# Expert results through DRAM rows, fetched once per token, in place of a one-hot scatter per expert

## The reference

```python
def _moe(h, w_router, w_gu, w_down):
    logits = jnp.einsum('bld,de->ble', h, w_router, preferred_element_type=jnp.float32)
    top_v, top_i = lax.top_k(logits, TOP_K)
    gates = jax.nn.softmax(top_v, axis=-1)
    comb = jnp.sum(jax.nn.one_hot(top_i, N_EXPERTS, dtype=jnp.float32) * gates[..., None], axis=-2)
    comb = comb.astype(h.dtype)
    out = jnp.zeros_like(h)
    for e in range(N_EXPERTS):
        out = out + comb[..., e:e + 1] * _swiglu(h, w_gu[e], w_down[e])
    return out
```

## Time and profile before

| | us |
|---|---|
| median of 3 runs (2141.97 to 2211.37) | 2142.83 |
| span of the profiled execution, first to last instruction | 2134.9 |
| median less span | 7.9 |
| PE busy in the span | 1923.1 (90%) |
| DVE busy | 1290.0 (60%) |
| ACT busy | 1091.2 (51%) |
| POOL busy | 130.0 (6%) |

### The profile page before, as it was taken

One profiled execution on the slowest core, in us unless ns is written; L12 is line 12 of the kernel. 1 busy time (PEld: TensorE's weight loads), 2 busy tenths in 40 slices (PEclk: granted clock), 3 DMA queues, 4 the chain that ended last, 5 costly groups with the idle time before them and its releaser, 6 DMA issues.

```text
span 2134.9 us, 27761 instructions
## 1 busy us (share of the span) xinstructions
PE 1923.1 (90%) x10133; PEld 1481.8 (69%) x10134; DVE 1290.0 (60%) x1580; ACT 1091.2 (51%) x1493; POOL 130.0 (6%) x202
## 2 busy tenths in 40 slices
PE   4778899989999989998799999999898989999992
PEld 3456676768888868776767576677677767777771
DVE  4754655553433262465366556588787868697775
ACT  3756533333332233563155445477676757676661
POOL 3010000000000050240000000000000000000001
PEclk7979995689999979998599999999999999999996
DMA  8946640024443444223067667699898979798871
GB/s 283 327 163 222 214 133 11 19 82 122 125 128 119 125 122 128 79 52 109 11 196 229 212 178 236 201 304 319 277 326 272 323 264 331 263 322 302 289 274 36
DMA packets 197611, 412.39 MB, mean 193 GB/s; under 512 B 16428, under 2 KB 35940, under 8 KB 197472
## 3 DMA queue, kind: packets, MB, share of 16 engines
q1 hardware_dynamic: 188928, 394.31, 55.9%
q0 software_dynamic: 8544, 16.14, 2.7%
HBM read 409.10 MB, written 4.33 MB: 194 GB/s over the span
## 4 chain that ended last, share of the span: by engine, by line
PE 73%; DVE 13%; ACT 6%; issue 4%; DMA 3%; POOL 0%; SPq 0%; ACTq 0%; DVEq 0%; POOLq 0%
PE ps L513 19%; PE ps L515 17%; PE ps L514 17%; DVE wlo L486 5%; PE ps L926 3%; DMA rawb<-in_mod_w 3%; PE ps L1096 2%; PE ps L1185 2%; ACT whi L482 2%; PE ps L958 2%; DVE wlo L463 2%; ACT whi L458 2%; PE ps L936 2%; PE ps L1201 1%; PE ps L1141 1%
## 5 line engine op out<-in xcount | busy, mean ns | idle before, releaser
L463 DVE TENSOR_TENSOR wlo<-rawb,whi 128x1024 fp32r<-128x1024 f32 x224 | 272.3, 1236 | 344.5 <-ACT whi L458 343.4
L486 DVE TENSOR_TENSOR wlo<-rawb,whi 128x1024 fp32r<-128x1024 f32 x288 | 347.5, 1222 | 173.9 <-ACT whi L482 172.6
L458 ACT ACTIVATE whi<-rawb 128x1024 fp32r<-128x1024 f32 x224 | 232.1, 1056 | 352.4 <-PE ps L515 319.4
L482 ACT ACTIVATE whi<-rawb 128x1024 fp32r<-128x1024 f32 x288 | 304.3, 1061 | 164.7 <-PE ps L515 87.1
L486 DVE TENSOR_TENSOR wlo<-rawx,whi 128x1024 fp32r<-128x1024 f32 x240 | 290.2, 1222 | 88.4 <-ACT whi L482 87.6
L513 PE MATMUL ps<-whi,eT_hi 128*128 128x512 f32 (+1 forms) x768 | 308.3, 401 | 31.9 <-issue 25.7
L482 ACT ACTIVATE whi<-rawx 128x1024 fp32r<-128x1024 f32 x240 | 252.6, 1061 | 119.0 <-PE ps L515 58.9
L514 PE MATMUL ps<-wlo,eT_hi 128*128 128x512 f32 (+1 forms) x768 | 292.3, 381 | 2.5 <-issue 2.5
L515 PE MATMUL ps<-whi,eT_lo 128*128 128x512 f32 (+1 forms) x768 | 291.0, 379 | 0.0
L513 PE MATMUL ps<-whi,hT_hi 128*128 128x512 f32 (+1 forms) x672 | 261.1, 389 | 20.9 <-DVE wlo L463 17.1
L515 PE MATMUL ps<-whi,hT_lo 128*128 128x512 f32 (+1 forms) x672 | 256.8, 382 | 0.0
(11 more groups left out here) (301 smaller groups left out, 2500.3 us busy)
## 6 DMA issues: line engine op xcount, KB each, us to landing
rawb<-in_od_moe_w_gu SPq DMA_DIRECT2D x192, 512.0 KB, 4.9
rawx<-in_od_moe_w_gu SPq DMA_DIRECT2D x160, 512.0 KB, 5.4
rawb<-in_mod_w SPq DMA_DIRECT2D x96, 512.0 KB, 5.5
rawb<-in_od_moe_w_down SPq DMA_DIRECT2D x96, 512.0 KB, 4.9
rawx<-in_od_moe_w_down SPq DMA_DIRECT2D x80, 512.0 KB, 4.9
rawb<-in_ev_ffn_w_gu SPq DMA_DIRECT2D x44, 512.0 KB, 3.7
rawb<-in_od_w_qkv SPq DMA_DIRECT2D x24, 512.0 KB, 3.9
rawb<-in_ev_w_in SPq DMA_DIRECT2D x22, 512.0 KB, 3.7
```

The lines of the kernel that those rows point to most:

```text
L458: nc.scalar.activation(whi[:, r, :], rawb[:, s, :], ACT.Copy).then_inc(hi_done, 1)
L463: nc.vector.tensor_tensor(wlo[:, r, :], rawb[:, s, :], whi[:, r, :].bitcast(F32), ALU.subtract).then_inc(lo_done, 1)
L482: nc.scalar.activation(whi[:, moe_slot(i), :], moe_raw(j), ACT.Copy).then_inc(hi_done, 1)
L486: nc.vector.tensor_tensor(wlo[:, moe_slot(i), :], moe_raw(i % EB), whi[:, moe_slot(i), :].bitcast(F32), ALU.subtract).then_inc(lo_done, 1)
```

## The change

The result of every expert goes to a DRAM scratch `rows_out`, the same way as the over rows. Each expert has PITCH = 416 rows there. ACT copies y once (`yr`, full float32), POOL stores it (512 KB), and at the end six indirect DMAs fetch for every token its two rows, all in bounds, two for each tile t, with a semaphore for each tile. DVE multiplies by the two weights and adds. Gone are `y_hi_t`, `y_lo_t`, `ohT`, `comb`, the six scatters and their additions, the transposes of `oh`, and the clearing of `acc`. The one-hot and the gather of the next expert move to earlier blocks, and the gather behind the last expert is dropped. New is that POOL clears the part of the scratch kept for more than 160 tokens, by 16 stores of 512 KB from a cleared `h[:, 0, :]`, issued once the rows of the dense SwiGLU's input have been transposed; DVE waits for them before it adds that SwiGLU's result to `x`.

```diff
-        SCATTER = {b: i for i, b in enumerate((4, 6, 8, 13, 15, 17))}
-        OH_TURN = GB + 5
-        ONE_HOT = GB + 10
-        GATHER = {GB + 12: 0, GB + 14: 1}
+        ONE_HOT = GB
+        GATHER = {GB + 8: 0, GB + 10: 1}
...
+            pool.wait_ge(tin_ps, 18)
+            nc.gpsimd.memset(h[:, 0, :], 0.0).then_inc(zeroed, 1)
+            pool.wait_ge(zeroed, 1)
+            for e in range(E):
+                for p in range(XT):
+                    o = e * PITCH + CAP + p * P
+                    pool.dma_start(rows_out[o:o + P, :], h[:, 0, :]).then_inc(zero_out, 16)
...
             for e in range(E):
+                o = e * PITCH
+                pool.wait_ge(y_ev, e + 1)
+                pool.dma_start(rows_out[o:o + P, :], yr[:, :]).then_inc(yr_out, 16)
                 pool.wait_ge(yo_ev, e + 2)
                 for g in range(4):
-                    pool.dma_start(over[e * OV:(e + 1) * OV, g * 2 * P:(g + 1) * 2 * P],
+                    pool.dma_start(rows_out[o + P:o + CAP, g * 2 * P:(g + 1) * 2 * P],
                                    yo[g * OV:(g + 1) * OV, :]).then_inc(yo_out, 16)
+            pool.wait_ge(yr_out, 16 * E)
             pool.wait_ge(yo_out, 64 * E)
+            pool.wait_ge(x_done, 1)
             pool.wait_ge(routed, 2)
-            for c in range(2):
-                for t in range(T):
-                    pool.indirect_dma_start(oy[:, c, t, :], None, over,
-                                            bass.IndirectOffsetOnAxis(ap=orow[:, c, t:t + 1], axis=0),
-                                            bounds_check=E * OV - 1, oob_is_err=False).then_inc(oy_in, 16)
+            for t in range(T):
+                for c in range(2):
+                    pool.indirect_dma_start(oy[:, c, t, :], None, rows_out,
+                                            bass.IndirectOffsetOnAxis(ap=orow[:, c, t:t + 1], axis=0)).then_inc(oy_in[t], 16)
...
                 def begin(b):
-                    if b in SCATTER:
-                        scatter_last(e, SCATTER[b])
-                    if b == OH_TURN:
+                    if b in GATHER and e + 1 < E:
                         pe.wait_ge(e_flo, e * NS + NS)
-                        for m in range(T):
-                            mm = nc.tensor.transpose(ps[:, 6, m * P:(m + 1) * P], oh[:, m, 0:P], ident)
-                        mm.then_inc(oht_ps, 1)
-                    if b in GATHER:
-                        pe.wait_ge(oht_ev, e + 1)
                         pe.wait_ge(oh_v, e + 2)
                         gather(GATHER[b]).then_inc(ga_ps, 1)
...
-            for i in range(6):
-                scatter_last(E, i, within=False)
-            pe.wait_ge(sc_v, E * 6 + 6)
+            pe.wait_ge(y_ev, E)
...
             def take_y(e):
                 act.wait_ge(pe_used, B_MOE + HL + e * EB)
-                nc.scalar.activation(y_hi_t[:, :], ps[:, 4:6, :].rearrange("p a n -> p (a n)"), ACT.Copy).then_inc(y_hi, 1)
+                if e > 1:
+                    act.wait_ge(yr_out, 16 * (e - 1))
+                nc.scalar.activation(yr[:, :], ps[:, 4:6, :].rearrange("p a n -> p (a n)"), ACT.Copy).then_inc(y_ev, 1)
...
+            take_y(E)
             take_over(E)
-            take_y(E)
...
-                    if b == Y_LAST:
-                        split_y(e)
-                    if b in SCATTER:
-                        scattered(e, SCATTER[b])
-                    if b == ONE_HOT:
-                        dve.wait_ge(oht_ev, e + 1)
+                    if b == ONE_HOT and e + 1 < E:
+                        dve.wait_ge(go_ps, e + 1)
                         one_hot(e + 1)
-                    if b in GATHER:
+                    if b in GATHER and e + 1 < E:
                         gathered(GATHER[b], e * 2 + 3 + GATHER[b])
...
+            dve.wait_ge(zero_out, 16 * XT * E)
...
             for t in range(T):
-                for c in range(2):
-                    chain(nc.vector.scalar_tensor_tensor(out=acc[:, t, :], in0=oy[:, c, t, :], scalar=gk[:, c, t:t + 1],
-                                                         in1=acc[:, t, :], op0=ALU.mult, op1=ALU.add))
+                dve.wait_ge(oy_in[t], 32)
+                chain(nc.vector.tensor_scalar(acc[:, t, :], oy[:, 0, t, :], gk[:, 0, t:t + 1], None, ALU.mult))
+                chain(nc.vector.scalar_tensor_tensor(out=acc[:, t, :], in0=oy[:, 1, t, :], scalar=gk[:, 1, t:t + 1],
+                                                     in1=acc[:, t, :], op0=ALU.mult, op1=ALU.add))
```

More of the change, by code:

```diff
@@ L56 @@
 XT = 2
-FAR = 1 << 20
+PITCH = CAP + XT * P
 MOD_CH, MOD_STEP = 12, 3
@@ L395, in build @@
         m_ld = [sem(f"m_ld{i}") for i in range(RM)]
-        y_hi = sem("y_hi")
-        y_lo = sem("y_lo")
+        zeroed = sem("zeroed")
+        zero_out = sem("zero_out")
+        y_ev = sem("y_ev")
+        yr_out = sem("yr_out")
         e_sg = sem("e_sg")
@@ L406, in build @@
         yo_out = sem("yo_out")
-        oy_in = sem("oy_in")
+        oy_in = [sem(f"oy_in{t}") for t in range(T)]
         x_oh = sem("x_oh")
-        x_go = sem("x_go")
+        x_go_pe = sem("x_go_pe")
+        x_go_act = sem("x_go_act")
         x_xp = sem("x_xp")
@@ L1106, in gather_over @@
                 return mm
-            def scatter(m, half):
-                o = ps[:, 6 + half, :]
-                yc = slice(512 * half, 512 * (half + 1))
-                nc.tensor.matmul(o, ohT[:, m * P:(m + 1) * P], y_hi_t[:, yc], start=True, stop=False)
-                return nc.tensor.matmul(o, ohT[:, m * P:(m + 1) * P], y_lo_t[:, yc], start=False, stop=True)
-            def scatter_last(e, i, within=True):
-                if i == 0:
-                    pe.wait_ge(y_lo, e + 1)
-                if i == 4 and within:
-                    pe.wait_ge(e_flo, e * NS + 1)
-                if i > 1 or not within:
-                    pe.wait_ge(sc_v, e * 6 + max(i - 1, 0))
-                scatter(i // 2, i % 2).then_inc(sc_ps, 1)
             def expert(e, more):
@@ L2070, in extra @@
                     conv(b)
-                dve.wait_ge(x_yhi, at(1, 1))
-                nc.vector.tensor_tensor(y_lo_t[:, :], ps[:, 4:6, :].rearrange("p a n -> p (a n)"),
-                                        y_hi_t[:, :].bitcast(F32), ALU.subtract).then_inc(x_ylo, 1)
-                for i in range(6):
-                    m, half = i // 2, i % 2
-                    cols = slice(512 * half, 512 * (half + 1))
-                    dve.wait_ge(x_sc, at(6, i + 1))
-                    nc.vector.scalar_tensor_tensor(out=acc[:, m, cols], in0=ps[:, 6 + half, :],
-                                                   scalar=comb[:, m, bass.ds(e + 1, 1)], in1=acc[:, m, cols],
-                                                   op0=ALU.mult, op1=ALU.add).then_inc(x_scv, 1)
             def route():
@@ L2102, in route @@
                 chain(nc.vector.tensor_copy(om[:, 1, :, :], m2[:, :, :]))
-                for t in range(T):
-                    chain(nc.vector.tensor_scalar(m1[:, t, :], m1[:, t, :], rt[:, 3, t:t + 1], None, ALU.mult))
-                    chain(nc.vector.scalar_tensor_tensor(out=comb[:, t, 1:], in0=m2[:, t, :], scalar=rt[:, 4, t:t + 1],
-                                                         in1=m1[:, t, :], op0=ALU.mult, op1=ALU.add))
+                chain(nc.vector.tensor_copy(gk[:, :, :], rt[:, 3:5, :]))
                 dve.wait_ge(pos_ps, 1)
```

113 lines of the change are left out of this document (33 added, 80 removed).

## The result

The changed kernel takes 2167.9 us (median of four executions, 2163.7 to 2170.4), against 2142.8 before. The ratio, with the two executions of the kernel before at 2211 left out, is 1.011 (95% interval 1.008 to 1.013): slower by 1.1% where 1.8% faster was forecast, 64 us above the forecast and outside its range. The profiled execution took 2163.72 with a span of 2162.0; before, 2134.9.

What follows compares the result with a forecast made beforehand. PE was taken to bound heavy experts and the down projection, PE and DVE light experts' blocks 0 to 20. Savings 6.1 + 17.75 + 9.55 + 0.4 + 4.6 = 38.4 us take 2142.8 to 2104; range 2093 to 2118.

Steps and rivals of the forecast that it cites:

- Clearing 8.4 MB: Stores of zeros during the dense SwiGLU, where PE is busy throughout: 34 us, all hidden, cost 0.
- The median above the span: Whole run: the median lies 7.9 us above the profiled span, an offset the change was said not to touch.
- heavy: Experts 0 and 1, which run the over rows: PE alone decides, 3.05 us saved each, 6.1 for both.
- light expert: Experts 2 to 7: each saves 3.55 us, 3.2 up to block 20 and 0.35 in the down projection.
- blocks 5 to 12: Light experts, two scatters and additions gone: 0.95 us saved, bounds 0.66 and 2.2.
- `one_hot` moved, first gather: Light experts' down projection: PE's wait for `oh` goes, a stall at block 47 may come; net 0, within 0.4.
- last expert, from its first `eg`: The last light expert saves 3.55 us and both useless gathers, 9.55 in all.
- router, norm 3 to the first `eg`: A chained clearing and a small operation leave DVE's path: about 0.4 us saved.
- sum starts earlier: Tail: DVE waits for two fetches instead of six, so the sum starts 2.8 us earlier.
- three one-input operations: Tail: one two-tensor operation per tile becomes one-tensor, 0.6 us saved each, 1.8 in all.
- Loads: Rival in the experts: weight loads become the bound; 2114 us in mild form, 2126 in full; chance 0.11.
- The rival of slow fetches: Tail: six fetches of valid rows set the end, 2109 us, at worst 2194; chances 0.08 and 0.04.

Runs made afterwards that it cites:

- the early Exp: One tiny unused Exp on ACT in the last QKV blocks: changed kernel 2098.6 to 2108.7 us (four), 2164 (two); kernel before 2200.9 to 2212.5.
- the filling in all waits: Small unread matmuls before every wait for exponentials in attention 1: changed kernel 2120.8 to 2127.1 us, ratio 0.991; kernel before 2170.5, 1.010.

## Why the prediction was wrong

**The step that failed** is "Clearing 8.4 MB ... Cost 0", with the silent assumption that a stage which the change doesn't touch keeps its time. Within its own stretch the step was right: from attention 0's last score product to norm 2, a stretch that holds the dense SwiGLU and the clearing, the profiles take 358.7 us (after) and 360.1 (kernel before with the clearing), and without it 360.0 (before) and 361.7 (clearing late). DMA view of after, and windows of its whole length:

```profile
rows_out_scratch<-h POOLq DMA_DIRECT2D x16, 512.0 KB, 10.3
```

```profile
460.00:480.00 20.00, 17.29 (x72) 13.30 (x71) 9.98 (x12) 6.88 (x9) 9.38 (x17) 0.87 0.67 249
480.00:500.00 20.00, 20.00 (x90) 16.57 (x89) 5.73 (x6) 8.16 (x9) 0.00 (x0) 1.00 0.88 329
500.00:520.00 20.00, 20.00 (x97) 16.62 (x95) 8.82 (x10) 5.22 (x6) 0.00 (x0) 1.00 0.39 108
```

It is over by 500 us, in some 34 us as estimated, and PE is busy for 20.0 of 20 us beside most of it. What it cost came 380 us later: attention 1 at clock 0.52, 59.9 us, and 4.7 more in the projection behind it. Shown is that the clearing at that place, alone, takes the high level from the kernel before (0 of 6 high-clock, against 10 of 12 when placed later and 54 of 79 without it), and that taking it away or moving it gives the changed kernel high-clock executions again (6 of 8, 4 of 8, against 0 of 10). Shown too is that more work for TensorE all through attention makes the level safe (18 of 18 executions of the four kernels with 51 or more extra matmuls there, 18 of 18 of the three with 28). The clearing shifts the odds and doesn't decide by itself: with the early Exp the changed kernel has the high clock in 4 of 6 although it clears at the old place, and the kernel before loses it in 6 of 6 without any clearing.

Not settled is by what path a transfer at 466 us reaches the clock at 878. No engine waits for it. But there is a row ahead of attention that goes with the level. These are the first 17.8 us behind the start of norm 2, some 100 us before attention 1, in the kernel before, the same with the clearing, and the changed kernel:

```profile
762.25:780.05 17.80, 14.26 (x43) 10.77 (x44) 10.91 (x12) 5.46 (x7) 13.59 (x20) 0.50 0.43 119
```

```profile
768.32:786.12 17.80, 13.58 (x50) 10.50 (x51) 10.91 (x12) 5.46 (x7) 13.50 (x21) 0.65 0.53 148
```

```profile
760.28:778.08 17.80, 13.49 (x50) 10.46 (x51) 10.91 (x12) 5.45 (x7) 13.40 (x21) 0.66 0.54 147
```

In the first the clock stays low all the while; in the other two it comes up once for a moment and falls again. Of the ten profiles with neither the early Exp nor the filling in all waits, the three with 0.50 here have attention 1 at the high clock and the seven with 0.63 to 0.66 have it at the low. With the early Exp it is the other way round (0.66 and high, 0.50 and low), and the filled kernels are high with either. That looks like theory A, an upstream edit that moves the moments at which the clock changes against the work, but it is one profile for each kernel, and no run set such a moment on purpose. The cause on this path stays open.

**The median above the span.** "7.9 above that span, which the change doesn't touch" is no property of the kernel: each execution lies 1.7 to 2.0 above its own span (2163.72 and 2162.0), and the rest was the difference between executions. It cost nothing here, since high-clock executions of the kernel before have medians of 2142 to 2150 by session, but the reason given was wrong.

**The other terms**, by the two profiles, from norm 3 on, where 38.4 was forecast. The pair gives 34.0. Over the profiles of seven versions of the kernel before and twelve of the changed one the medians are 1133.1 and 1096.1: 37.0. The changed kernel with the early Exp has 1091.9: 37.9 less than before. That this comes so near to 38.4 is in part luck: as the table shows, the first expert and the tail gave less than forecast, the router more, and the light experts more for a reason that the sum doesn't have.

| step | predicted | measured |
|---|---|---|
| expert 0 to expert 1 (heavy) | 3.05 | -2.8 in this pair (169.0 to 171.8); 163.5 to 171.8 in all profiles, by the length of a stretch at clock 0.5 inside it |
| expert 1 to expert 2 (heavy) | 3.1 | 2.8 (153.3 to 150.5) |
| light expert | 3.55 | 4.4 (583.8 to 561.9 over five); 4.1 by the medians of all profiles |
| blocks 5 to 12 | 0.95 | 0.64, the lower bound |
| blocks 13 to 20 | 1.73 | 1.73 |
| `one_hot` moved, first gather | 0 | +0.64 - 0.43 = 0.2 saved |
| last expert, from its first `eg` | 9.05 | 6.9 in this pair (94.5); 8.5 (101.4 to 92.9) between executions without the slip of 1.5 us named at the end |
| router, norm 3 to the first `eg` | 0.4, and 0.45 of expert 0's first scatter | 4.0 in this pair (76.7 to 72.7), 2.5 by the means of all (75.0, 72.5) |
| sum starts earlier | 2.8 | 0.5 |
| three one-input operations | 1.8 | 1.4 |
| behind the sum | 0 | -0.6 |

The three rows below "light expert" are parts of it.

- *Light experts.* The mechanism holds: even distances and PE's ring as the limit. DVE's part in blocks 5 to 12 was hidden altogether, so the lower bound was the value. The first gather's 0.64 was PE's wait for `oh`, as supposed, and the stall at block 47 is 0.43: they nearly cancel, as counted, though the stall is a little beyond the 0.4 named as a sign of being wrong. Ahead of the first `eg`, where `y_lo_t` and block 4's scatter went and 0.5 was taken, an undisturbed expert saves 0.4 (9.33 to 8.91 from its first product). All this makes 3.3. The rest of the 4.1 is no work removed: the distance between the last two copies of `eg` is 13.0 in place of 11.5 us in 26 of 42 light experts of the kernel before and in 19 of 72 of the changed one, some 0.5 us on the mean, and longer stretches ahead of the first `eg` (12.28 in one expert of before) are rarer too. Why, no run shows. The 5 us in which PE waits for its instructions are still 4.3 to 5.4.
- *Loads.* The rival is out: 0.90 of DMA, 314 GB/s and no wait, though POOL's store of y now stands in the same stretch. The turns between queues that the Trainium skill describes under "DMA: Bandwidth & Descriptors", section "Queues, rings and completion order", don't show in the time here: gate and up loads land in 5.3 and 5.6 us by their medians over the run, against 4.9 and 5.4 before, well inside the ring's lead of an estimated 12.
- *Router.* The gain is there at either level of attention 1 (low-clock: 76.5 in the kernel before with the clearing, 72.7 in the changed one). It has three parts. DVE comes to the one-hot 0.7 sooner (39.98 and 39.26 us behind norm 3), where 0.4 was taken. The scatter in front of expert 0's block 4 goes, 0.45. And in the gather of the over rows PE waited for its instructions twice in the kernel before and once in the changed one, a wait that the prediction didn't have:

```profile
1055.73 0.85 PE L1104 MATMUL ps<-oh,h 128*128 128x32 f32 x6 [2.45 <-issue]
1058.97 8.96 PE L1104 MATMUL ps<-oh,h 128*128 128x32 f32 x42 [2.39 <-issue]
```

```profile
1115.99 9.37 PE L1104 MATMUL ps<-oh,h 128*128 128x32 f32 x48 [2.12 <-issue]
```

  The second wait, 2.1 to 2.4 us, is in four of the seven profiles of the kernel before and in one of twelve of the changed one; what brings it is not shown.
- *Tail.* The last product ends at 2117.61 and the first fetch is issued at 2125.96, 8.35 later, against 5.97 before: 2.4 more, where 1.3 was taken. The stores that have to land took 4.13 instead of 2.96. The fetch of valid rows took 5.39, against 3.01 for one of dropped rows: 2.4 more, where 1.4 was taken. The second was within its bounds, the first at its upper one (1.06 + 1.3), both on the dear side, and together they used up nearly all that waiting for two fetches instead of six gave. The tiles are 4.80 and 4.50 apart; the one-input operation takes 0.68 as estimated, but 0.98 the first time. The rival of slow fetches is out: all tiles behind the first were hidden.

## What to carry to other kernels

Before costing a change, look at the granted clock of every long stretch and at the spread of the runs shown: two groups of executions 68 us apart can mean that a stage sits between two clock levels, and an edit upstream, even a hidden one, can shift which it gets; give that its own chance. Compare such kernels stage by stage, or hold the clock in both with cheap work on TensorE, before judging the change. Work put beside a busy TensorE can be free where it stands and still cost elsewhere, so move it and see: in the kernel before, the same stores were free behind attention and went with 60 us more ahead of it.

## What was not expected of the hardware

- Attention 1 runs at 2.4 GHz for its whole length, or falls to 1.2 GHz within 5 to 12 us of its start and stays there until it ends: 78 to 79.4 us, or 135 to 140. No profile of an unfilled kernel shows anything between.
- Work added to a stretch made it faster: the slowest execution of the changed kernel with 28 small matmuls more in attention 1 (and 92 in attention 0) took 2105.9, the fastest without them 2163.7. Attention 0 went from 64.0 us to 57.3 to 59.9 with 92 matmuls more.
- Writing 8.4 MB to DRAM at 466 to 500 us changed the odds of the granted clock at 878.
- The last distance between copies of `eg` in a light expert is 11.51 or 13.02 us, now the one and now the other in both kernels, so single profiles of an expert differ by 1.5 us; the longer one is more frequent in the kernel before.
